# Prompt attention tiles of two heads side by side, values of both heads issued in alternation

## What is computed

```python
q = (rmsnorm(cq, qnorm_g) @ w_uq).reshape(B, L, MLA_HEADS, MLA_NOPE + MLA_ROPE)
kv = (ckv_all @ p['w_ukv'][l]).reshape(B, ckv_all.shape[1], MLA_HEADS, MLA_NOPE + MLA_V)
k_nope, v = kv[..., :MLA_NOPE], kv[..., MLA_NOPE:]

def mla_attend(q_nope, q_pe, q_pos, k_nope, k_pe, v, k_pos):
    s = jnp.einsum('bqhd,bkhd->bhqk', q_nope, k_nope) + jnp.einsum('bqhr,bkr->bhqk', q_pe, k_pe)
    s = s.astype(jnp.float32) * MLA_SCALE
    mask = (k_pos[None, :] // CHUNK) <= (q_pos[:, None] // CHUNK)
    s = jnp.where(mask[None, None], s, -jnp.inf)
    p = jax.nn.softmax(s, axis=-1).astype(v.dtype)
    return jnp.einsum('bhqk,bkhv->bqhv', p, v)
```

## Time and profile before

| | us |
|---|---|
| median of 3 runs | 2846.68 |
| lowest, highest | 2845.35, 2848.07 |
| profiled execution, own time | 2847.45 |
| profiled execution, span | 2845.7 |
| mean granted clock of TensorE | 0.959 of 2.4 GHz |

### The profile page before, as it was taken

The page is one execution under the profiler, slowest core; times in us unless marked ns, Lnnn a source line. Parts: engine busy times, 40 slices in busy tenths (PEclk is TensorE's granted clock), DMA queues, the critical chain, the costliest instruction groups (busy, mean ns, idle before and its releaser), DMA issues. The chain is left out here.

```text
span 2845.7 us, 43077 instructions
## 1 busy us (share of the span) xinstructions
PE 2606.2 (92%) x17236; PEld 2415.6 (85%) x17236; DVE 1630.0 (57%) x2810; ACT 1086.6 (38%) x1852; POOL 432.4 (15%) x182
## 2 busy tenths in 40 slices
PE   5699999989889969999969999998997996999997
PEld 1399999989777869999969999998986786999997
DVE  2574655553675387473777456366257537737474
ACT  1342342432344254252444334244333434525242
POOL 0002020233210101102120201114321010020202
PEclk8899999989999979999989999998998998999999
DMA  8443433322241012222224334242214100222222
GB/s 325 190 157 109 134 126 111 134 72 75 73 129 41 31 45 97 67 89 75 90 74 140 120 126 139 100 141 79 82 39 147 64 31 30 90 75 89 75 89 83
DMA packets 81473, 283.22 MB, mean 100 GB/s; under 512 B 10016, under 2 KB 12992, under 8 KB 80640
## 3 DMA queue, kind: packets, MB, share of 16 engines
q1 hardware_dynamic: 70848, 257.25, 26.7%
q10 hardware_dynamic: 10432, 23.27, 2.7%
HBM read 274.03 MB, written 6.46 MB: 99 GB/s over the span
## 5 line engine op out<-in xcount | busy, mean ns | idle before, releaser
L1035 PE MATMUL bank<-t_hi,w_hi 128*128 128x320 f32 x2464 | 779.1, 316 | 93.8 <-DVE t_lo L1573 86.2
L1036 PE MATMUL bank<-t_lo,w_hi 128*128 128x320 f32 x2464 | 767.6, 312 | 0.0
L1037 PE MATMUL bank<-t_hi,w_lo 128*128 128x320 f32 x2464 | 767.3, 311 | 0.0
L459 POOL TENSOR_TENSOR w_lo<-raw,w_hi 128x1024 fp32r<-128x1024 f32 x160 | 393.0, 2461 | 2197.1 <-ACT w_hi L499 2197.1
L1035 PEld LDWEIGHTS bank<-t_hi,w_hi 128*128 128x128 f32 x2464 | 468.8, 190 | 140.8 <-DVE t_lo L1573 89.7
L1036 PEld LDWEIGHTS bank<-t_lo,w_hi 128*128 128x128 f32 x2464 | 469.3, 190 | 0.0
L1037 PEld LDWEIGHTS bank<-t_hi,w_lo 128*128 128x128 f32 x2464 | 468.7, 190 | 0.0
L993 PE MATMUL bank<-h_hi,w_hi 128*128 128x320 f32 x1408 | 436.4, 310 | 2.4 <-DVE h_lo L1742 1.9
L995 PE MATMUL bank<-h_hi,w_lo 128*128 128x320 f32 x1408 | 435.1, 309 | 0.0
L994 PE MATMUL bank<-h_lo,w_hi 128*128 128x320 f32 x1408 | 435.0, 309 | 0.0
L499 ACT CAST w_hi<-raw 128x1024 fp32r<-128x1024 f32 x160 | 167.4, 1050 | 317.1 <-PE bank L995 296.6
(11 more groups left out here) (263 smaller groups left out, 4173.5 us busy)
## 6 DMA issues: line engine op xcount, KB each, us to landing
raw<-in_wmain SPq DMA_DIRECT2D x336, 512.0 KB, 3.6
araw<-in_wada SPq DMA_DIRECT2D x144, 512.0 KB, 4.7
pk_t<-in_pastkT ACTq DMA_DIRECT2D x16, 256.0 KB, 4.0
pv<-in_pastv ACTq DMA_DIRECT2D x16, 256.0 KB, 4.3
x<-in_xT SPq DMA_DIRECT2D x1, 2560.0 KB, 14.9
y<-y_sb SPq DMA_DIRECT2D x1, 2560.0 KB, 7.5
s_s<-in_s ACTq DMA_DIRECT2D x4, 512.0 KB, 3.8
uk_t<-in_ukT ACTq DMA_DIRECT2D x2, 1024.0 KB, 6.4
```

The source lines that it names most:

```text
L459: pool.tensor_tensor(w_lo[slot][:], raw[slot % 2][:].rearrange("p (c m) -> p c m", m=P), w_hi[slot][:].bitcast(F32), ALU.subtract).then_in ...
L1035: pe.matmul(out, hi, t_hi[i][:, c, :], start=first and c == 0, stop=False, skip_group_check=True)
L1036: pe.matmul(out, hi, t_lo[i][:, c, :], start=False, stop=False, skip_group_check=True)
L1037: mm = pe.matmul(out, lo, t_hi[i][:, c, :], start=False, stop=(c == 3), skip_group_check=True)
```

## The change

Prompt tile 8 + j becomes head 2 (j // 8) + j % 2, query tile (j % 8) // 2: both heads of a pair at query tile 0, then both at 1, and so on, so that widths run 1, 1, 2, 2, 3, 3, 4, 4. V of the first tile of each such two is not issued in its turn; the turn of the second issues the matmuls of both, one of the even head, one of the odd head, over k. There are 16 signals `pv_mm` in a layer in place of 32, and a fourth pt_p buffer, which lies over pt_s. The products with w_uv alternate between two heads after each matmul in place of after two.

```diff
--- before.py
+++ after.py
@@ -186,7 +186,7 @@
         pt_s = [in_a(f"pt_s{i}", [P, 3, P], 36864 + 1536 * i) for i in range(2)]
         cn_t = in_a("cn_t", [P, KL * P], 39936)
         o_lat = in_a("o_lat", [P, KL, MH, P], 0)
-        pt_p = [in_a(f"pt_p{i}", [P, 4, P], 30720 + 2048 * i) for i in range(3)]
+        pt_p = [in_a(f"pt_p{i}", [P, 4, P], 30720 + 2048 * i) for i in range(4)]
 
         v_g = in_b("v_g", [P, 5, GH * GV], 0)
         q_sub = in_b("q_sub", [P, 2, NT], 10240)
@@ -292,7 +292,7 @@
         gv_mm = signal("gv_mm", 4)
         lat_mm = signal("lat_mm", 4)
         lat_mm_sq = signal("lat_mm_sq", 2)
-        pv_mm = signal("pv_mm", 32)
+        pv_mm = signal("pv_mm", 16)
         att_mm = signal("att_mm", 4)
         kdt_mm = signal("kdt_mm", 4)
         ds_mm = signal("ds_mm", 8)
@@ -389,6 +389,11 @@
                      dict(A=0, AS=6, KT=1, KTS=(4, 0), DS=(2, 3), DSS=(1, 4), O=(5, 7, 0), ST=(2, 3, 6)))
         QBANKS = ((1, 4), (2, 3), (6, 5), (7, 0)) * 2
         SBANKS, TBANKS = (6, 5, 2, 3), (7, 0)
+
+        def prompt_tile(it):
+
+            j = it - NDEC
+            return 2 * (j // 8) + j % 2, (j % 8) // 2
 
         def out_tile(l, f, p, m):
             return l * OUT_T + f * (3 * DC + MIX_T) + p * DC + m
@@ -923,7 +928,7 @@
                                                       b[:, PAST:PAST + DSEQ], ACT.Exp, bias=mx[:, n:n + 1],
                                                       accum_out=psum2[:, n:n + 1]))
                         else:
-                            w = P * ((it - NDEC) % 4 + 1)
+                            w = P * (prompt_tile(it)[1] + 1)
                             if it >= NDEC + 4:
                                 t_mm.wait(act, l, it - 4)
                             if it in (NDEC, NDEC + 2):
@@ -939,10 +944,12 @@
                                 ol_mm.wait(act, l, jt - 2)
                             pt_out.send(act.copy(pt_s[jt % 2][:], b[:, 0:3 * P].rearrange("p (c t) -> p c t", t=P)))
                         else:
-                            qt = (jt - NDEC) % 4
-                            if jt >= NDEC + 3:
-                                pv_mm.wait(act, l, jt - NDEC - 3)
-                            pt_out.send(act.copy(pt_p[jt % 3][:, 0:qt + 1, :],
+                            qt = prompt_tile(jt)[1]
+                            if jt >= NDEC + 4:
+                                pv_mm.wait(act, l, (jt - NDEC - 4) // 2)
+                            elif jt == NDEC + 3:
+                                ol_mm.wait(act, l, 7)
+                            pt_out.send(act.copy(pt_p[jt % 4][:, 0:qt + 1, :],
                                                  b[:, 0:P * (qt + 1)].rearrange("p (c t) -> p c t", t=P)))
                     if NPB <= it + 4 < NDEC:
                         load_keys(it + 4)
@@ -953,7 +960,7 @@
                         ohi_out.send(act.copy(o_hi[:, 4:8, SEQ:NT], bank[1][:, :].rearrange("p (c t) -> p c t", t=P)))
                     hp = (it - 5 - NDEC - 7) // 8
                     if it == NDEC + 8 * hp + 12 and 0 <= hp < 4:
-                        pv_mm.wait(act, l, 8 * hp + 7)
+                        pv_mm.wait(act, l, 4 * hp + 3)
                         ohi_out.send(act.copy(o_hi[:, 4 + hp, 0:SEQ], bank[(4, 1)[hp % 2]][:, :]))
 
                 for m in range(DC):
@@ -1414,7 +1421,7 @@
                         s_mm.send(pe.matmul(b[:, PAST:PAST + DSEQ], q, kg[:, new], start=False, stop=True,
                                             skip_group_check=True))
                     else:
-                        h, qt = (it - NDEC) // 4, (it - NDEC) % 4
+                        h, qt = prompt_tile(it)
                         if it == NDEC:
                             kpe_copied.wait(pe, l, 0)
                         w = P * (qt + 1)
@@ -1428,14 +1435,14 @@
                         pt_out.wait(pe, l, it - 2)
                     else:
                         vm_out.wait(pe, l, 2 + it)
-                    src, n = (p_s[it % 4], 3) if it < NDEC else (p_p[it % 4], (it - NDEC) % 4 + 1)
+                    src, n = (p_s[it % 4], 3) if it < NDEC else (p_p[it % 4], prompt_tile(it)[1] + 1)
                     for c in range(n):
                         mm = pe.transpose(b[:, c * P:(c + 1) * P], src[:, c * P:(c + 1) * P], ident[:])
                     t_mm.send(mm)
 
                 def values(it):
-                    pt_out.wait(pe, l, it)
                     if it < NDEC:
+                        pt_out.wait(pe, l, it)
                         b = bank[(1, 4)[it % 2]]
                         if it >= 2:
                             ol_out.wait(pe, l, it - 2)
@@ -1451,16 +1458,20 @@
                                                start=(k == 0), stop=(k == 2))
                         ol_mm.send(mm)
                         return
-                    h, qt = (it - NDEC) // 4, (it - NDEC) % 4
-                    hp, r0 = h // 2, MV * (h % 2)
-                    if h % 2 == 0 and qt == 0:
+                    if it % 2 == 0:
+                        return
+                    pt_out.wait(pe, l, it)
+                    h, qt = prompt_tile(it)
+                    hp = h // 2
+                    if qt == 0:
                         sg, w = ((ol_out, 7), (olo, 4), (olo, 5), (olo, 6))[hp]
                         sg.wait(pe, l, w)
                     for k in range(qt + 1):
-                        mm = pe.matmul(bank[(4, 1)[hp % 2]][r0:r0 + MV, qt * P:(qt + 1) * P],
-                                       v_m[:, k, h * MV:(h + 1) * MV], pt_p[it % 3][:, k, :], start=(k == 0), stop=(k == qt))
+                        for e in range(2):
+                            mm = pe.matmul(bank[(4, 1)[hp % 2]][MV * e:MV * e + MV, qt * P:(qt + 1) * P],
+                                           v_m[:, k, (2 * hp + e) * MV:(2 * hp + e + 1) * MV],
+                                           pt_p[(it - 1 + e) % 4][:, k, :], start=(k == 0), stop=(k == qt))
                     pv_mm.send(mm)
-                    return mm
 
                 for it in range(40 + 4):
                     if 3 <= it < 43:
@@ -1473,11 +1484,10 @@
 
                         ol_out.wait(pe, l, 7)
                         pe.wait_ge(uv_in, 16 * l + 16)
-                        for h in range(MH):
-                            for c in range(KL):
-                                mm = pe.matmul(bank[1][MV * (h % 2):MV * (h % 2) + MV, (h // 2) * P:(h // 2 + 1) * P],
-                                               w_uv[:, c, h * MV:(h + 1) * MV], o_lat[:, c, h, :],
-                                               start=(c == 0), stop=(c == KL - 1))
+                        for c, h in ((c, h + e) for h in range(0, MH, 2) for c in range(KL) for e in range(2)):
+                            mm = pe.matmul(bank[1][MV * (h % 2):MV * (h % 2) + MV, (h // 2) * P:(h // 2 + 1) * P],
+                                           w_uv[:, c, h * MV:(h + 1) * MV], o_lat[:, c, h, :],
+                                           start=(c == 0), stop=(c == KL - 1))
                         uv_mm.send(mm)
 
                 for m in range(DC):
@@ -2064,7 +2074,7 @@
                             t = p_s[n][:]
                         else:
                             own(dve.reciprocal(rsum[:, n:n + 1], psums[:, n:n + 1]))
-                            t = p_p[n][:, 0:P * ((jt - NDEC) % 4 + 1)]
+                            t = p_p[n][:, 0:P * (prompt_tile(jt)[1] + 1)]
                         p_norm.send(dve.tensor_scalar(t, t, rsum[:, n:n + 1], None, ALU.mult))
                     jo = it - 4
                     if 0 <= jo < NDEC:
```

## The result

The changed kernel takes 2834.08 us (median of 5 runs, 2830.36 to 2837.22), the kernel before 2848.07 (median of 5 runs). The ratio is 0.9949, 95% interval 0.9938 to 0.9961: 14.0 us faster, at least 0.39% and at most 0.62%. The forecast was 15.8 us.

The account below looks back on a forecast made before the run. TensorE closely sets the loop's pace. Steady pair 14.94 - 3.54 + 1.86 + 0.1 = 13.36 us; pairs save 3.6 + 1.9 + 1.6 + 0.8 = 7.9 per layer, 15.8 in all, giving 2831.0 us, range 2822 to 2840.

Parts of the forecast that it names:

- What bounds the kernel: Prompt attention loops: TensorE sets the pace, closely, busy 14.18 of 14.94 us; only these 140 us can change.
- Values of two heads together: Values matmuls in the loop: overlapping column halves and four fewer groups remove 3.54 us per pair, 14.2 per layer.
- Reordered w_uv products, nothing: w_uv products at L1478: both halves are already in use at 0.056 us per pass, so no gain.
- Order of the tiles: Steady pair: transposes wait longer for the norm behind VectorE's max, taking back 1.86 us per pair.
- the walk: Tile-by-tile timing of the loop from measured lengths and lags; waits of 3.10 us per pair, 1.24 in the old order.
- Cast and o_lo stretch the wait ahead of the first T of 384: Transposes at width 3: the previous pair's cast (0.61) and o_lo (0.69) ahead of the max raise 0.33 to 1.10 us.
- First and last pair: Loop ends: first pair from 18.4 to 14.8 us, last with the tail from 20.7 to 19.9.
- o_lat's wait would go: First pair: the 1.58 us wait goes, as the next values stand a turn later and the max before the copy is narrower.
- Costed at nothing: Fourth pt_p buffer over pt_s and 16 signals for 32: the added wait of the copies is never the last one.
- The halves do not overlap: Rival, values matmuls: passes keep 0.109 us, only switches go; pair 15.3, loop 69.35, time 2846, no change; chance 0.07.
- The chain does not bind: Rival, loop waits: they are mis-sized and the removed work arrives whole, about 2816 us; chance 0.05.
- The clock falls: Rival, loop: thinner TensorE work lowers the granted clock, slower, 2876 us if it fell for good; chance 0.05.

Follow-up runs that it names:

- run on one half: Changed kernel with both heads of a pair writing their values to the same column half, head after head: 2845.88 us, 0.9985 of the kernel before.
- blocks run: Changed kernel with both alternations undone, values and w_uv products going head after head within their groups: 2845.38 us in one run, loops 65.29 and 65.01.
- score first: Changed kernel with each turn's score issued ahead of transposes and values from turn 12: 2817.4 us, 0.9882; same edit in the kernel before: 2836.5 us, 0.9947.
- second reciprocal: Changed kernel with the reciprocal of each prompt tile done twice on VectorE: 2843.9 us in one run, loops 64.69 and 64.38.
- order run: Changed kernel's tile order and four pt_p buffers, but each head's values alone in their own turn, with 32 signals: 2845.46 us, 0.9985 of the kernel before.
- doubled reciprocal in the old kernel: Kernel before the change with the reciprocal of each prompt tile done twice: 2852.8 us in one run, loops 73.27 and 73.01.
- run by twos: Changed kernel with values alternating after two matmuls (four passes) per head: 2841.98 us in one run, loops 62.71 and 62.43.
- run with the cast later: Changed kernel with each pair's cast to o_hi and its o_lo one turn later: 2831.63 us, 0.9930 of the kernel before.

## Why the prediction was right

- **What bounds the kernel**, and that only the loops could change: they gave 15.85 us, the forecast said 15.8. The forecast time of 2831.0 lies 3.1 below the measured median, within the scatter of the part outside the loops; the median of before moved as well, by 1.4 us, as more of its runs came in. (By the sum's own terms the forecast is 2830.9.)
- **Values of two heads together**: groups of 4, 8, 12, 16 passes last 0.44, 0.66, 0.88, 1.09 for the 0.49, 0.71, 0.92, 1.14 I gave. The 0.05 too much is a mis-sized detail: the halves' passes start 0.006 to 0.007 apart, where I let them alternate at half the spacing. The run on one half shows that this term carries the gain.
- **Reordered w_uv products, nothing**: 1.97 for 2.02, right. Against the program order of the Trainium skill ("TensorE: Matmul & The Clock Gate", Part 3) I set the row of L1478 as if it held for any order. The runs show a rule between the two: three waiting passes may be passed over. L1478 had blocks of four and could not tell. (The 2.65 that I gave for strict order leaves out the 0.27 to the end of the last pass: about 2.9, and 0.9 for the 0.6.) My sum did not fail by it because the change alternates in V, but my expectation of the blocks run did.
- **Order of the tiles**, the term that takes 1.86 per pair back: the walk gave waits of 0.14, 0.45, 1.10 and 1.06 ahead of T and 0.32 ahead of V; the rows show idle of 0.29, 0.91 and 0.89 for the three larger ones and 0.25 for V (the idle time starts at the end of the pass before, 0.16 to 0.19 later, for V 0.07, than the point from which the walk counts), and a pair of 13.34 for 13.36. No idle shows for the smallest, 0.14, as the end of the pass before covers it. That these waits are the chain over VectorE is shown from two sides: score first takes 5.6 of the 8.7 us away, the second reciprocal adds 2.5 (11.2 in its list).
- **Cast and o_lo stretch the wait ahead of the first T of 384**: shown by moving them one turn.
- **First and last pair**: 14.97 for 14.8, 19.90 for 19.9. The second pair of layer 0 took 14.28 where layer 1 took 13.96 as forecast; the surplus sits in the wait ahead of the first T of 384 (1.23 for 0.90). VectorE starts the first max of 384 0.3 us later in layer 0, after an idle time that no releaser ends; why it idles there stays open. That o_lat's wait would go: right, the reason half wrong, as the order run showed. The rows of that max in layer 0 and in layer 1:

```profile
896.73 0.56 DVE L2064 TENSOR_REDUCE mx<-bank 128x1 f32<-128x384 f32 x1 [0.23 <-issue]
...
2253.53 0.55 DVE L2064 TENSOR_REDUCE mx<-bank 128x1 f32<-128x384 f32 x1
```

- **Costed at nothing**: in ScalarE's own waits of layer 0's loop the copy to pt_p waits for the transposes alone (1.9 us), never for V. No run changes the fourth buffer or the number of signals by itself, so that they cost nothing is shown by this list alone.
- **The rivals.** *The halves do not overlap*: out (1.09). The run on one half gives 69.7 for the 69.35 worked out for it. *The chain does not bind*: out; with score first it binds less, 2.25 of the 3.54 us removed arrive. *The clock falls*: not in the changed kernel, 1.00 in both loops, though TensorE is busy 11.00 of 13.34. It was a real danger for single stretches, as the doubled reciprocal in the old kernel showed: its price there, 1.5 to 1.6 us per fall, is near the 1.7 I had taken. A fall in the tail, which I had left room for, is absent behind both loops of this profile and present at the end of both in the run by twos, whose loop is only 0.2 us longer.

## What to carry to other kernels

Matmuls with 64 columns of weights (here f32, 128 by 64, with 128 columns moving) cost half when work for both column halves stands close together in TensorE's queue: alternate them, or keep blocks to two f32 matmuls. Before counting the gain, walk the chain that feeds TensorE: here 3.54 us removed per pair became 1.6, because the next transposes then waited for VectorE. The remedy was to issue the producer of that chain (the score) first in its turn, at which no run here shows a cost, and which was worth nearly as much as the change itself: 6.5 us per loop by itself for 7.9, 7.6 on top of the change. Both together give 0.9882.

## What I had not expected of the hardware

- TensorE starts a pass of the idle column half ahead of up to three passes of the other half that stand before it: blocks of four passes per half overlap (0.66 us for 8 passes, as when alternating), blocks of six and eight lose 0.27 and 0.49 us, and on one half alone 16 passes take 1.96.
- A wait of 1.78 us in TensorE was followed by 3.4 us at half the granted clock in one kernel, while 1.58 us at the same place in another was not; the fall cost 1.5 to 1.6 us. In the profiled execution with score first a like fall stands just behind each loop, within the output projection; there TensorE had waited 1.46 us. The changed kernel waited as long at the same place and kept 1.00; the run with the cast later fell to 0.50 behind its first loop, the run by twos at the end of both. What TensorE's waits alone do to the clock these traces do not settle. The stretch behind the first loop with score first:

```profile
926.50:929.90 3.40, 3.40 (x14) 3.40 (x15) 0.02 (x1) 0.00 (x0) 0.00 (x0) 0.50 0.00 0
```
